# Convolution's layer norm: six taps move to TensorE, ScalarE evicts, and the variance is handled as 128x4 columns

## The reference

```python
def layernorm(x, g, b):
    mu = mean(x, -1); var = mean(square(x - mu), -1)
    return (x - mu) * rsqrt(var + EPS) * g + b

def conformer_conv(x, norm_g, pw1_w, pw1_b, dw_w, dw_b, ln_g, ln_b, pw2_w, pw2_b):
    a, b = split(rmsnorm(x, norm_g) @ pw1_w + pw1_b, 2)
    h = a * sigmoid(b)
    h = depthwise_conv(h, dw_w, 31 taps, causal) + dw_b
    h = silu(layernorm(h, ln_g, ln_b))
    return h @ pw2_w + pw2_b
```

## Time and profile before

| | |
|---|---|
| Time, median of 3 runs | 2720.51 us (2719.8 to 2720.86) |
| Profiled execution | 2722.52 us, span 2720.7 us |
| Mean granted TensorE clock | 0.98 |
| TensorE busy | 2603.9 us, 96% of the span |
| VectorE busy | 1430.1 us, 53% |
| ScalarE busy | 946.1 us, 35% |
| Chain that ended last, by engine | TensorE 84%, VectorE 10%, ScalarE 3% |
| Taps on VectorE (L847) in the chain | 3% of the span |

### The profile page before, as it was taken

One profiled execution on the slowest core, in us unless ns is written; L12 is line 12 of the kernel. 1 busy time (PEld: TensorE's weight loads), 2 busy tenths in 40 slices (PEclk: granted clock), 3 DMA queues, 4 the chain that ended last, 5 costly groups with the idle time before them and its releaser, 6 DMA issues.

```text
span 2720.7 us, 34006 instructions
## 1 busy us (share of the span) xinstructions
PE 2603.9 (96%) x12132; PEld 2122.1 (78%) x12132; DVE 1430.1 (53%) x2139; ACT 946.1 (35%) x1659; POOL 372.8 (14%) x313
## 2 busy tenths in 40 slices
PE   6988999999999999999998898999999999999999
PEld 5866888877777788888777786788878877688887
DVE  5896444435787544443443565544434656544422
ACT  5454332223466323222333434332222124333221
POOL 2003000011166400012100040200011050300000
PEclk9999999999999999999998998999999998999999
DMA  4202333223200232322321022233323332133322
GB/s 147 78 1 62 94 99 93 81 97 128 82 1 1 63 100 93 98 79 93 115 72 32 16 95 60 80 98 95 92 86 107 95 95 93 55 100 93 96 97 70
DMA packets 61149, 219.82 MB, mean 81 GB/s; under 512 B 7152, under 2 KB 7408, under 8 KB 60672
## 3 DMA queue, kind: packets, MB, share of 16 engines
q1 hardware_dynamic: 58896, 209.15, 24.8%
q0 software_dynamic: 2160, 9.44, 1.0%
HBM read 216.47 MB, written 2.10 MB: 80 GB/s over the span
## 4 chain that ended last, share of the span: by engine, by line
PE 84%; DVE 10%; ACT 3%; issue 1%; POOL 1%; ACTq 0%; DMA 0%; DVEq 0%; SPq 0%; POOLq 0%
PE psum L212 24%; PE psum L214 24%; PE psum L213 24%; DVE conv_out L847 3%; DVE wl L195 2%; PE psum L1904 2%; PE psum L1881 1%; ACT wh L189 1%; PE psum L1210 1%; PE psum L1158 1%; DVE x L743 1%; PE psum L2713 1%; PE psum L2109 1%; PE psum L1864 1%; PE psum L1863 1%
## 5 line engine op out<-in xcount | busy, mean ns | idle before, releaser
L212 PE MATMUL psum<-xh,wh 128*128 128x512 f32 x1880 | 739.0, 393 | 32.1 <-DVE wl L195 23.5
L213 PE MATMUL psum<-xl,wh 128*128 128x512 f32 x1880 | 735.2, 391 | 0.0
L214 PE MATMUL psum<-xh,wl 128*128 128x512 f32 x1880 | 735.0, 391 | 0.0
L189 ACT ACTIVATE wh<-raw 128x1024 fp32r<-128x1024 f32 x404 | 421.6, 1057 | 783.3 <-PE psum L214 777.1
L195 DVE TENSOR_TENSOR wl<-raw,wh 128x1024 fp32r<-128x1024 f32 x404 | 551.7, 1378 | 145.6 <-ACT wh L189 143.0
L212 PEld LDWEIGHTS psum<-xh,wh 128*128 128x128 f32 x1880 | 354.4, 189 | 108.0 <-issue 24.0
L214 PEld LDWEIGHTS psum<-xh,wl 128*128 128x128 f32 x1880 | 354.1, 188 | 75.9 <-issue 0.8
L213 PEld LDWEIGHTS psum<-xl,wh 128*128 128x128 f32 x1880 | 354.6, 189 | 74.5 <-issue 0.6
L212 PE MATMUL psum<-hidden_high,wh 128*128 128x512 f32 x704 | 276.5, 393 | 4.3 <-DVE wl L195 3.8
L213 PE MATMUL psum<-hidden_low,wh 128*128 128x512 f32 x704 | 274.2, 390 | 0.0
L214 PE MATMUL psum<-hidden_high,wl 128*128 128x512 f32 x704 | 274.0, 389 | 0.0
(11 more groups left out here) (381 smaller groups left out, 3288.6 us busy)
## 6 DMA issues: line engine op xcount, KB each, us to landing
raw<-ffn_in SPq DMA_DIRECT2D x176, 512.0 KB, 3.5
raw<-ffn_out SPq DMA_DIRECT2D x64, 448.0 KB, 4.2
raw<-ffn_out SPq DMA_DIRECT2D x32, 512.0 KB, 3.6
raw<-pw SPq DMA_DIRECT2D x24, 512.0 KB, 3.5
raw<-o_w_hgg SPq DMA_DIRECT2D x12, 512.0 KB, 4.2
raw<-w_q SPq DMA_DIRECT2D x8, 512.0 KB, 3.6
raw<-w_o SPq DMA_DIRECT2D x8, 512.0 KB, 3.5
raw<-e_w_qk SPq DMA_DIRECT2D x8, 512.0 KB, 3.5
```

The source lines that it names most:

```text
L189: self.nc.scalar.activation(self.wh[:, slot, :], self.raw[:, slot, :], ACT.Copy).then_inc(self.weights_high.sem, 1)
L212: nc.tensor.matmul(out, ah, bh, start=start, stop=False)
L213: nc.tensor.matmul(out, ah, bl, start=False, stop=False)
L214: return nc.tensor.matmul(out, al, bh, start=False, stop=stop)
```

## The change

- `OURS` goes from 12 to 9: VectorE has three taps fewer for each of tiles 4 and 5, TensorE and ScalarE's diagonals have six more (106).
- ScalarE evicts all four of TensorE's sums with the bias added (`evict`, an Identity activation). Those of tiles 4 and 5 it evicts in the midst of the diagonals, before VectorE's first tap of the tile, and VectorE then adds its nine taps to what ScalarE wrote. Those of tiles 6 and 7 follow the last diagonal.
- The mean's products take the tiles in the order 0 to 3, 6, 7, 4, 5.
- The variance's products have the squares as the stationary operand and one column of 1/1024 as the moving one: four products of one column for each tile in place of one with 512. The result is 128x4, tokens on the partitions.
- Root and inverse are of 128x4. Four products of a broadcast column with the identity spread the inverse root over 128x512 in PSUM bank 4.
- VectorE scales by that bank alone, and the weight column goes into the silu as its scale. ScalarE copies the high part of tile m right behind the silu of tile m, and VectorE makes the low part one tile behind.

```diff
-    OURS = 12
+    OURS = 9
...
-        self.root = c.arena("conv_root", 84, [P, S])
-        self.rs = c.arena("conv_rstd", 86, [P, S])
+        self.rs = c.arena("conv_rstd", 82.5, [P, 2 * NT])
...
-            if k == 0:
+            if k == 0 and pair != self.SHARED:
                 dve.tensor_scalar(out, taps, w, c.col("dw_b", m), ALU.mult, ALU.add).then_inc(self.tapped.sem, 1)
             else:
-                dve.wait_ge(self.tapped.sem, n - 1)
+                if k == 0:
+                    dve.wait_ge(self.moved.sem, m - 4 + 1)
+                else:
+                    dve.wait_ge(self.tapped.sem, n - 1)
                 dve.scalar_tensor_tensor(out, taps, w, out, ALU.mult, ALU.add).then_inc(self.tapped.sem, 1)
...
+            for t in self.SHARED:
+                if n == (t - 3) * (TAPS - self.OURS) + self.SLOTS_OF_TAPS:
+                    self.evict(act, t)
...
+    def evict(self, act, m):
+        c = self.c
+        act.wait_ge(self.pe_tapped.sem, sum(1 for t, k in self.theirs if t <= m))
+        act.activation(self.out[:, m, :], c.psum[:, m, :], ACT.Identity, bias=c.col("dw_b", m)).then_inc(
+            self.moved.sem, 1)
...
-        for k, m in enumerate(self.SHARED):
-            dve.wait_ge(self.pe_tapped.sem, (k + 1) * (TAPS - self.OURS))
-            dve.tensor_tensor(self.out[:, m, :], c.psum[:, 4 + k, :], self.out[:, m, :], ALU.add).then_inc(
-                self.moved.sem, 1)
-        for k, m in enumerate(self.WHOLE):
-            dve.wait_ge(self.pe_tapped.sem, 2 * (TAPS - self.OURS) + (k + 1) * TAPS)
-            dve.tensor_scalar(self.out[:, m, :], c.psum[:, 6 + k, :], c.col("dw_b", m), None, ALU.add).then_inc(
-                self.moved.sem, 1)
...
-        dve.reciprocal(self.rs[:], self.root[:]).then_inc(self.centred.sem, 1)
-        dve.wait_ge(self.centred.sem, KD + 1)
-        dve.wait_ge(self.sq_done.sem, KD)
+        dve.reciprocal(self.rs[:, NT:2 * NT], self.rs[:, 0:NT]).then_inc(self.centred.sem, 1)
+        dve.wait_ge(self.ln_stat.sem, 3)
         for m in range(KD):
-            dve.scalar_tensor_tensor(self.out[:, m, :], self.out[:, m, :], c.col("ln_g", m), self.rs[:],
-                                     ALU.mult, ALU.mult).then_inc(self.ln_scaled.sem, 1)
-            if m >= 2:
-                self.low(dve, m - 2)
-        self.low(dve, KD - 2)
+            dve.tensor_tensor(self.out[:, m, :], self.out[:, m, :], c.psum[:, 4, :], ALU.mult).then_inc(
+                self.ln_scaled.sem, 1)
+            if m >= 1:
+                self.low(dve, m - 1)
         self.low(dve, KD - 1)
...
+        for m in self.WHOLE:
+            self.evict(act, m)
...
-        act.activation(self.root[:], c.psum[:, self.var_bank, :], ACT.Sqrt, bias=c.eps[:]).then_inc(
+        act.activation(self.rs[:, 0:NT], c.psum[:, self.var_bank, 0:NT], ACT.Sqrt, bias=c.eps[:]).then_inc(
             self.ln_root.sem, 1)
         act.preload_act_table(ACT.Silu)
-        for m in range(KD + 1):
-            if m < KD:
-                act.wait_ge(self.ln_scaled.sem, m + 1)
-                act.activation(self.out[:, m, :], self.out[:, m, :], ACT.Silu, bias=c.col("ln_b", m)).then_inc(
-                    self.silu_done.sem, 1)
-            if m >= 1:
-                act.wait_ge(self.silu_done.sem, m)
-                act.activation(self.parts[0][:, m - 1, :], self.out[:, m - 1, :], ACT.Copy).then_inc(self.high.sem, 1)
+        for m in range(KD):
+            act.wait_ge(self.ln_scaled.sem, m + 1)
+            act.activation(self.out[:, m, :], self.out[:, m, :], ACT.Silu, bias=c.col("ln_b", m),
+                           scale=c.col("ln_g", m)).then_inc(self.silu_done.sem, 1)
+            act.wait_ge(self.silu_done.sem, m + 1)
+            act.activation(self.parts[0][:, m, :], self.out[:, m, :], ACT.Copy).then_inc(self.high.sem, 1)
...
-        for m in range(KD):
-            if m < 4:
-                pe.wait_ge(self.tapped.sem, 2 * TAPS * (m // 2 + 1))
+        for m in (0, 1, 2, 3, *self.WHOLE, *self.SHARED):
+            if m in self.WHOLE:
+                pe.wait_ge(self.moved.sem, m - 4 + 1)
             else:
-                pe.wait_ge(self.moved.sem, m - 4 + 1)
+                pe.wait_ge(self.tapped.sem, len(self.ours) if m in self.SHARED else 2 * TAPS * (m // 2 + 1))
             mm = pe.matmul(c.psum[:, self.mean_bank, :], c.sq["mean"][:], self.out[:, m, :], start=(m == 0),
-                           stop=(m == KD - 1))
+                           stop=(m == self.SHARED[1]))
...
             pe.wait_ge(self.sq_done.sem, m + 1)
-            pe.matmul(c.psum[:, self.var_bank, :], c.sq["mean"][:], self.sq[:, m % 4, :], start=(m == 0),
-                      stop=(m == KD - 1)).then_inc((self.ln_stat if m == KD - 1 else self.sq_used).sem, 1)
+            for i in range(NT):
+                mm = pe.matmul(c.psum[:, self.var_bank, i:i + 1], self.sq[:, m % 4, i * P:(i + 1) * P],
+                               c.sq["mean"][:, 0:1], start=(m + i == 0), stop=(m == KD - 1 and i == NT - 1),
+                               skip_group_check=True)
+            mm.then_inc((self.ln_stat if m == KD - 1 else self.sq_used).sem, 1)
+        pe.wait_ge(self.centred.sem, KD + 1)
+        for i in range(NT):
+            mm = pe.matmul(c.psum[:, 4, i * P:(i + 1) * P], self.rs[:, NT + i:NT + i + 1].to_broadcast([P, P]),
+                           c.sq["ident"][:], start=True, stop=True, skip_group_check=True)
+        mm.then_inc(self.ln_stat.sem, 1)
```

## The result

The changed kernel takes 2725.32 us (median of 20 runs, 2719.84 to 2732.92) against 2720.93 us (20 runs, 2718.36 to 2725.18). The ratio is 1.0018, with a 95% interval of 1.0012 to 1.0024: 4.4 us or 0.18% slower, where 2718.3 us and a gain of 2.2 were forecast. Its profiled execution took 2727.63 us with a span of 2725.8. The median is outside the range of 2713.5 to 2721.6. Among all executions behind this document three took 2951.71 to 4388.78 us at a mean granted clock of 0.56 to 0.84, and the ratios leave them out, as does the row of the delay of 3.47 us.

The account below looks back on a forecast made before the run. The prediction took the convolution's chain of waits up to pw2's unbroken products as the bound. The mean gained 4.3 us, the variance gave most back, the end stretch counted zero: 2.2 us gained, 2718.3 us, range 2713.5 to 2721.6.

Parts of the forecast that it names:

- What bounds the kernel: Chain of waits through the convolution to pw2's unbroken products; moving their start moves the kernel's end by as much.
- Taps and evictions: Convolution's taps to mean: VectorE ends at 190.0, evictions of 0.70 us hidden, mean at 195.24, 4.3 us gained.
- Variance: 64 one-column passes after the mean: clock falls at 199.7, products end at 207.38 against 208.13 before.
- the middle of three rows: Clock falls 3.1, 4.6 and 4.9 us after dense products in the trace; the middle one puts the variance's fall at 199.7.
- no row shows fewer than 3.0: Argument against rival 2: its threshold is a clock fall 2.4 us after dense work, sooner than any row showed.
- rival 2: Clock falls before the convolution's variance starts: first scaling 0.8 us later than before, 2721.3 us; chance 0.12.
- Root, inverse, spread: Between variance and first scaling: 0.30, 0.22 and 2.11 us, first scaling at 210.03 instead of 212.26.
- Scaling, silu, split: From first scaling to pw2's eighth product: 12.28 us as before, so zero change, within 0.5 either way.
- a ring through VectorE: In scaling, silu and split: 0.71 + 0.75 + 0.65 + 0.61 = 2.72 us for two tiles; ScalarE alone 1.27 for one.
- Sum: Whole kernel: gain of 2.2 us taken from the median 2720.51, giving 2718.3 us.
- the last part: Stretch from first scaling to pw2's eighth product, forecast at 12.28 us, unchanged within 0.5.

Follow-up runs that it names:

- the delay of 3.47 us: Kernel before plus eight needless VectorE copies behind the inverse root, nothing else changed: 2724.62 us, ratio 1.0012 (1.0002 to 1.0021).
- the taps part: Nine taps, ScalarE's evictions and the mean's order alone, variance to silu as in the kernel before: 2722.07 us, ratio 1.0009 (0.9996 to 1.0022).
- a bare delay of 0.69 or 1.66 us: Kernel before plus two or four needless VectorE copies behind the inverse root: 2725.39 us in both runs of 0.69, 2726.59 us for 1.66.
- the fourth profile: Changed kernel with the old order of silu and copy, weight still in the silu: 2724.35 us, ratio 1.0014 (1.0005 to 1.0023).

## Why the prediction was wrong

*What bounds the kernel.* Right about the stage. Wrong in one sentence, on which the sum rested: that whatever moves the start of pw2's unbroken run moves the end by as much. This is the larger part of the error. The end moved by 4.4 us for 0.9 us; the taps part moved the start by 4.2 us and the end not at all. What stood in its place: the rest of the kernel has sparse stretches, the norms' one-column products above all, and whether and for how long the clock falls at one depends on when the stretch comes, and differs between executions. The earlier trace rows had shown such falls, and they were read as a price inside the convolution only. Shown: the time behind the convolution goes with the time at half clock, wider products at the norms take it back in both kernels, and a bare delay of 0.69 or 1.66 us brings a loss of this size. Not shown: which later arrival is a good one, and how much falls to the attention parts, which gave 1.4 of the 4.7 us in the profiles and were left as they are.

*Taps and evictions.* Right to 0.1 us: first centring 195.37 against 195.27, taps end 189.5 (190.0 with the head start) against 190.0, eviction 0.69, nothing waits for ScalarE.

*Variance.* The mechanism was right, its size was not. The term is the fall of the clock: 199.7 was taken, the middle of three rows; it fell at 197.2, 197.1 and 197.6 in three profiles, and at 200.0 in a fourth. With 56 passes at half pace the 64 take 13.0 us, not the 10.7 of the sum: 2.3 us. (The full pace was 0.112 us a pass and not the 0.106 of the earlier trace rows, which is worth little for eight passes.) That "no row shows fewer than 3.0" was true of the four falls that were looked at and not of the trace of the kernel before. TensorE's last dense pass ahead of 1368 us ends at 1365.6 there, and the clock falls at 1368.2, 2.6 us behind it; ahead of that, after a dense pass that ends at 1355.5, it falls at 1357.9:

```profile
1365.22 0.40 PE L214 MATMUL psum<-xh,wl 128*8 128x512 f32 x1
```

```profile
1365.70:1368.00 2.30, 0.00 (x0) 0.00 (x0) 1.20 (x2) 1.06 (x1) 0.00 (x0) 1.00 0.00 0
1368.00:1369.00 1.00, 0.33 (x3) 0.33 (x4) 0.61 (x2) 0.00 (x0) 0.00 (x0) 0.59 0.00 0
```

Both falls came in full pauses, so they don't settle the case of sparse passes, but with them a fall 2.4 us after dense work, rival 2's side, had deserved more than a chance of 0.12. Why the clock fell at 200.0 in the fourth profile, 5.3 us after the mean's last pass, is open.

*Root, inverse, spread.* Root to first scaling 2.64 us (209.39 to 212.03), 2.63 forecast.

*Scaling, silu, split.* 12.85 us against 12.28: 0.6 us off, and outside the 0.5 allowed. The sum had a ring through VectorE of 2.72 us for two tiles, and 1.27 a tile for ScalarE alone. In the chain from 212.76 to 224.11 it is ScalarE alone that sets the pace, silu and copy in turn, 2.83 for two tiles. The silu with a scale column as well as a bias is 0.81 long in place of 0.72, which is 0.2 of the 0.6 by the kernels with and without it; the other 0.4 is the order, which the sum had put at nothing against the old one.

*Sum.* With 2.3 and 0.6 us more than the forecast's terms, and 0.2 of small differences, the convolution is 0.9 us later and not 2.2 earlier. That this is nearly rival 2's 0.8 is in part luck: its variance ends 0.6 us later than the measured one, and it has not the 0.6 of the last part. The remaining 3.5 us of the median arise behind the convolution; with the norms' products widened in both kernels they are gone. The upper end of the range, 2721.6, is also 0.2 below its own terms, 2721.3 and 0.5; that changes nothing here.

*The rules of the Trainium skill.* TensorE's row is busy throughout over 197 to 203 us with one column and with 128; the clock is 0.52 in the first kernel and 1.00 in the second. The Trainium skill (TensorE: Matmul & The Clock Gate, section "What's actually happening") says that the gate follows how busy TensorE has been; the busy row of the profile does not tell these two kernels apart. A one-column pass with its own weights took 0.112 us at full clock. The 25 ns that the Trainium skill gives on the same page for a narrow matmul (section "Back-to-back issue gap") did not show.

## What to carry to other kernels

Cutting the moving columns of a product to one saved nothing here, where each pass brings its own weights (0.112 us with one column and with 128, at full clock), and halved TensorE's clock, there and in what follows: give such products the columns that cost nothing. A saving of a few microseconds ahead of sparse TensorE stretches can be given back at these, far away; before judging it, make them dense in both kernels, or time the old kernel with bare delays. The useful version here has 128 columns in the convolution's and the norms' products, the old order of silu and copy, and the weight in VectorE's product from PSUM: 2712.35 us, 9.1 us below the kernel before. Of these the wider norms alone give the old kernel 2.9.

## What the runs showed of the hardware

- 64 float32 passes with a weight load each: 7.41 us with 128 moving columns, at full clock; with one column 13.0 to 13.2 where the clock fell after some 8 passes, 10.3 and 10.4 where it fell halfway. A one-column pass takes 0.112 us at full clock and 0.213 at half.
- The clock fell 2.5 and 2.6 us after the end of dense work where TensorE paused (1357.9 and 1368.2 in the profile of before), and 2.2 to 2.4 us after it at one-column passes in three profiles, 5.3 and 5.4 in two.
- A silu of 128x512 takes 0.72 us with a bias column and 0.81 with a scale column too.
- In four profiles of kernels that are the same up to the variance, the clock fell within it at 197.1, 197.2 and 197.6 us after the start, and at 200.0. That such falls keep nearly the same time in most executions would explain why medians over executions did not hide the effect of a shift; it was not tried.
